# A pipelined scan on one core: the state phase of the second group one slot forward, turned inverses at the end of a half step

## The reference

```python
def step(S, inp):
    r_t, w_t, k_t, v_t, a_t, b_t = inp
    sa = jnp.einsum('zdhij,zdhj->zdhi', S, a_t)
    S = S * w_t[..., None, :] + sa[..., :, None] * b_t[..., None, :] + v_t[..., :, None] * k_t[..., None, :]
    y = jnp.einsum('zdhij,zdhj->zdhi', S, r_t)
    return S, y
```

## Time and profile before

| | us |
|---|---|
| median of 3 runs | 2615.3 (2611.9 to 2617.37) |
| the profiled execution, its own time | 2613.51 |
| its span | 2611.6 |
| TensorE busy | 2464.9 (94%), 28048 instructions |
| TensorE weight loads busy | 2047.2 (78%) |
| VectorE busy | 1210.7 (46%) |
| ScalarE busy | 720.4 (28%) |
| GpSimd busy | 819.8 (31%) |

### The profile page before, as it was taken

How to read it: one execution, slowest core, us unless ns; L and a number is a source line. 1 busy time by engine, 2 the same in 40 slices (tenths; PEclk the granted TensorE clock), 3 DMA queues, 4 the chain that set the end, 5 groups by cost and what they waited for, 6 DMA issues and landing times. The chain is left out here.

```text
span 2611.6 us, 63691 instructions
## 1 busy us (share of the span) xinstructions
PE 2464.9 (94%) x28048; PEld 2047.2 (78%) x28048; DVE 1210.7 (46%) x2468; ACT 720.4 (28%) x1799; POOL 819.8 (31%) x627
## 2 busy tenths in 40 slices
PE   7999999999999599999989989999999999999997
PEld 6785568888888488888777867878888888888885
DVE  4105660000555356566666565554444444444446
ACT  5115651111111355555545432210111001110013
POOL 3322122222332233324333265022333323323234
PEclk9999999999999699999999989999999999999999
DMA  6110011111110100000000052211111111111114
GB/s 165 45 33 18 1 50 73 65 73 73 41 33 25 43 4 4 4 4 4 4 4 4 4 231 92 97 57 35 47 41 41 33 33 49 41 41 33 33 65 145
DMA packets 39087, 123.11 MB, mean 47 GB/s; under 512 B 11424, under 2 KB 11424, under 8 KB 37664
## 3 DMA queue, kind: packets, MB, share of 16 engines
q1 hardware_dynamic: 38816, 119.06, 13.4%
HBM read 96.24 MB, written 20.97 MB: 45 GB/s over the span
## 5 line engine op out<-in xcount | busy, mean ns | idle before, releaser
L2037 DVE TENSOR_TENSOR ff_f<-ff_f,ff_ps 128x512 f32<-128x512 f32 x300 | 205.6, 687 | 173.5 <-PE ff_ps L98 173.5
L1954 ACT ACTIVATE ff_rl<-ff_ps 128x512 f32<-128x512 f32 (+1 forms) x96 | 50.6, 527 | 756.3 <-PE ff_ps L98 756.3
L2056 DVE TENSOR_TENSOR ff_sq<-ff_rl 128x512 f32<-128x512 f32 (+1 forms) x96 | 126.1, 1314 | 273.0 <-ACT ff_rl L1954 272.6
L1823 POOL TENSOR_TENSOR ff_wd0h<-ff_wdr,params 128x1024 fp32r<-128x1024 f32 x16 | 30.3, 1895 | 460.7 <-DMA ff_wdr<-in_w_down 460.7
L996 DVE TENSOR_TENSOR sc_q<-sc_ps,sc_cs 128x128 f32<-128x128 f32 x400 | 97.1, 279 | 163.3 <-PE sc_ps L420 161.4
L436 PE MATMUL sc_ps<-sc_xy,sc_q 64*64 64x64 f32 x3200 | 157.4, 222 | 2.0 <-DVE sc_q L996 1.6
L751 ACT ACTIVATE sc_xy<-sc_ps 128x256 f32<-128x256 f32 x320 | 119.2, 387 | 136.5 <-PE sc_ps L436 134.0
L98 PE MATMUL ff_ps<-hh,ff_wu0h 128*128 128x512 f32 (+1 forms) x384 | 137.0, 357 | 4.7 <-issue 4.7
L432 PE MATMUL sc_ps<-sc_q,sc_xy 64*64 64x64 f32 x2560 | 116.3, 236 | 24.4 <-ACT sc_xy L746 17.4
L98 PE MATMUL ff_ps<-hh,ff_wu0l 128*128 128x512 f32 (+1 forms) x384 | 136.9, 356 | 0.0
L98 PE MATMUL ff_ps<-hl,ff_wu0h 128*128 128x512 f32 (+1 forms) x384 | 136.9, 356 | 0.0
(11 more groups left out here) (306 smaller groups left out, 7059.3 us busy)
## 6 DMA issues: line engine op xcount, KB each, us to landing
ff_wur<-in_w_up SPq DMA_DIRECT2D x32, 512.0 KB, 3.5
ff_wdr<-in_w_down SPq DMA_DIRECT2D x32, 512.0 KB, 4.4
gwr<-in_w_in SPq DMA_DIRECT2D x31, 512.0 KB, 3.2
gm_dram<-gp_gm SPq DMA_DIRECT2D x8, 1280.0 KB, 4.4
ff_m<-gm_dram SPq DMA_DIRECT2D x16, 640.0 KB, 8.2
fr_x<-in_x SPq DMA_DIRECT2D x10, 512.0 KB, 5.4
ff_xs<-in_x SPq DMA_DIRECT2D x10, 512.0 KB, 4.1
x_dram<-ff_xo SPq DMA_DIRECT2D x10, 512.0 KB, 2.9
```

The lines of the kernel that those rows point to most:

```text
L1823: nc.gpsimd.tensor_tensor(high, w_raw[m], zero_like(high, zero), ALU.add).then_inc(high_done, 1)
L1954: nc.scalar.activation(rl[v % 2][:, 0:tn], ps[:, b, 0:tn], ACT.Relu).then_inc(relu, 1)
L2037: nc.vector.tensor_tensor(own, own, ps[:, 4 + v % 4, :], ALU.add).then_inc(added, 1)
L2056: nc.vector.tensor_tensor(sq[v % 2][:, 0:tn], rl[v % 2][:, 0:tn], rl[v % 2][:, 0:tn], ALU.mult).then_inc(squared, 1)
```

## The change

Six things are done, and the arithmetic stays as it is.

1. The two turned inverses of a half step leave its beginning. They are issued at the end of the half step before, behind the last X/Y product; those of the first half step are issued ahead of the loop.
2. Both are copied by one ScalarE instruction. For that the X/Y tiles of two groups lie in one tensor (XYS), and `flipped` counts pairs.
3. The state phase of the second group (sb) moves one slot forward on TensorE, ScalarE and VectorE: state_in ahead of Q of level 2, solved ahead of X/Y of level 2, state_out behind it, outputs behind Q of level 3; VectorE's `state` and `collect` stand in level 3, not 4.
4. The first Q products of both groups stand together, and solved of the group sa stands behind both first X/Y. The gram product of sa stands ahead of Q of level 2, that of sb ahead of Q of level 4; the tokens of sa stand before solved, those of sb before the last X/Y.
5. Side products of piece 1 go from spot 2 to a new spot 5, between outputs and X/Y of level 3; their VectorE half goes from level 4 to 3.
6. The second of the two running sums of the decays goes from level 3 of an odd half step to level 0 of the next one.

```diff
@@ -163,7 +163,8 @@
-        XY = [sb(f"sc_xy{g}", [P, 2, 2, C]) for g in range(GR)]
+        XYS = [sb(f"sc_xy{h}", [P, HALF, 2, 2, C]) for h in range(2)]
+        XY = [XYS[g // HALF][:, g % HALF, :, :, :] for g in range(GR)]
...
+        flips_out = ps[:, GRAM_BANK, 0:HALF * C].rearrange("p (g t) -> p g t", g=HALF)
...
                 if l == 0:
-                    pe.wait_ge(flipped, q * GR + g + 1)
+                    pe.wait_ge(flipped, q * 2 + g // HALF + 1)
...
                     if spot == 2:
                         piece_out(ct, i, 2, GRAM_BANK)
+                    if spot == 5:
                         piece_out(ct, i, 1, TOK_BANK)
...
-                    if spot == 2 and ct + 1 < CT:
+                    if spot == 5 and ct + 1 < CT:
                         pe.wait_ge(sqk_ready, (ct + 2) * NG)
                         by_head(TOK_BANK, nrm, ss_ps)
...
@@ -595,17 +600,15 @@
                 if levels:
                     level_q(q, 0, ga)
+                    level_q(q, 0, gb)
                 if inner:
                     state_in(qs, sa)
                 if levels:
-                    level_q(q, 0, gb)
-                    flip(q, ga)
-                    flip(q, gb)
                     level_xy(q, 0, ga)
+                    level_xy(q, 0, gb)
                 if inner:
                     solved(qs, sa)
                 if levels:
-                    level_xy(q, 0, gb)
                     pe.wait_ge(tok_ready, q * GR + gb + 1)
...
                 if inner:
                     state_in(qs, sb_)
                 if levels:
-                    level_xy(q, 2, gb)
+                    level_q(q, 2, ga)
+                    level_q(q, 2, gb)
                 side(t, 1)
                 if more:
                     by_token(qa, sa)
+                if inner:
+                    solved(qs, sb_)
+                if levels:
+                    level_xy(q, 2, ga)
+                    level_xy(q, 2, gb)
+                if inner:
+                    state_out(qs, sb_)
+                if more:
+                    pe.wait_ge(masked, qa * GR + sa + 1)
+                side(t, 2)
                 if levels:
                     level_q(q, 3, ga)
                     level_q(q, 3, gb)
                 if inner:
-                    solved(qs, sb_)
+                    outputs(qs, sb_)
                 if more:
-                    pe.wait_ge(masked, qa * GR + sa + 1)
                     pe.wait_ge(tok_ready, qa * GR + sa + 1)
-                side(t, 2)
+                side(t, 5)
                 if levels:
                     level_xy(q, 3, ga)
                     level_xy(q, 3, gb)
...
                 if more:
                     gram_products(qa, sb_)
                 if levels:
-                    level_xy(q, 4, ga)
-                    level_xy(q, 4, gb)
+                    level_q(q, 4, ga)
+                    level_q(q, 4, gb)
                 side(t, 4)
                 if more:
                     by_token(qa, sb_)
+                if levels:
+                    level_xy(q, 4, ga)
+                    level_xy(q, 4, gb)
+                if t + 1 < PAIRS:
+                    flip(qa, sa)
+                    flip(qa, sb_)
...
-            def flip_copy(q, g):
-                act.wait_ge(flip_ps, q * GR + g // HALF * HALF + HALF)
-                nc.scalar.activation(XY[g][:, Y_AT, 1, :], flip_out[g], ACT.Copy).then_inc(flipped, 1)
+            def flip_copy(q, h):
+                act.wait_ge(flip_ps, q * GR + h * HALF + HALF)
+                nc.scalar.activation(XYS[h][:, :, Y_AT, 1, :], flips_out, ACT.Copy).then_inc(flipped, 1)
...
+                    if l == 0 and late:
+                        cumulate(q + 1, 1)
...
                     if l == 2 and more:
                         start_group(qa, sa)
-                    if l == 1 and ahead:
-                        half(q + 2, 0)
+                    if l == 3 and inner:
+                        state(qs, sb_)
+                        collect(qs, sb_)
+                    if l == 3:
+                        side(t, 2, GRAM_BANK)
+                        side(t, 1, TOK_BANK)
                     if l == 3 and ahead:
                         half(q + 2, 1)
                         cumulate(q + 2, 0)
-                        cumulate(q + 2, 1)
...
```

More of the change, by code:

```diff
@@ L587, in _ @@
             pe.wait_ge(ta_ready, 2)
+            flip(0, 0)
+            flip(0, 1)
             for t in range(PAIRS + 1):
@@ L617, in _ @@
                     state_out(qs, sa)
+                    outputs(qs, sa)
                 if levels:
@@ L620, in _ @@
                     level_xy(q, 1, gb)
[L621 to L625, removed]
                 if ahead:
@@ L629, in _ @@
                     gram_products(qa, sa)
-                if levels:
-                    level_xy(q, 2, ga)
                 if inner:
@@ L650, in _ @@
                     level_xy(q, 3, gb)
[L651 to L657, removed]
                 side(t, 3)
@@ L777, in _ @@
             decays(1, 1)
+            flip_copy(0, 0)
             for t in range(PAIRS + 1):
@@ L792, in _ @@
                 if levels:
-                    flip_copy(q, ga)
-                    flip_copy(q, gb)
                     level_copy(q, 0, ga)
+                    level_copy(q, 0, gb)
                 if inner:
                     u_copy(qs, sa)
-                if levels:
-                    level_copy(q, 0, gb)
-                if inner:
                     keep(qs, sa)
@@ L804, in _ @@
                     lora_tanh(q + 2, 1)
+                if squares_y and t % 2:
+                    y_square(ct - 1, 1)
                 if levels:
@@ L809, in _ @@
                     decays(q + 1, 0)
[L810 to L813, removed]
                 if inner:
                     p_copy(qs, sb_)
-                if levels:
-                    level_copy(q, 2, gb)
+                    keep(qs, sb_)
                 if more:
@@ L820, in _ @@
                 if inner:
-                    keep(qs, sb_)
+                    u_copy(qs, sb_)
+                if levels:
+                    level_copy(q, 2, ga)
+                    level_copy(q, 2, gb)
                 if late:
@@ L825, in _ @@
                     y_square(ct - 1, 0)
-                if inner:
-                    u_copy(qs, sb_)
-                if levels:
-                    level_copy(q, 3, ga)
-                    level_copy(q, 3, gb)
                 if squares_y and t % 2:
@@ L834, in _ @@
                     k_norm(ct + 1, TOK_BANK)
+                if levels:
+                    level_copy(q, 3, ga)
+                    level_copy(q, 3, gb)
+                if squares_y and t % 2 == 0:
+                    y_square(ct - 1, 2)
                 if squares_k:
@@ L837, in _ @@
                         k_square(ct + 1, p)
+                if more:
+                    token_copy(qa, sb_)
                 if levels:
                     level_copy(q, 4, ga)
-                if squares_y and t % 2 == 0:
-                    y_square(ct - 1, 2)
-                if levels:
                     level_copy(q, 4, gb)
-                if more:
-                    token_copy(qa, sb_)
+                if t + 1 < PAIRS:
+                    flip_copy(qa, sa // HALF)
             def high_half(ct):
@@ L1058, in _ @@
                         collect(qs, sa)
+                    if l == 1 and ahead:
+                        half(q + 2, 0)
                     if l == 2 and more:
                         start_group(qa, sa)
-                    if l == 1 and ahead:
-                        half(q + 2, 0)
+                    if l == 3 and inner:
[4 more added lines that the diff above has]
+                        side(t, 1, TOK_BANK)
                     if l == 3 and ahead:
@@ L1065, in _ @@
                         cumulate(q + 2, 0)
-                        cumulate(q + 2, 1)
-                    if l == 3:
-                        side(t, 2, GRAM_BANK)
-                    if l == 4:
-                        side(t, 1, TOK_BANK)
-                    if l == 4 and inner:
-                        state(qs, sb_)
-                        collect(qs, sb_)
                     if l == 4 and more:
```

## The result

The changed kernel takes 2619.2 us at the median (2615.6 to 2630.1, 14 runs), the kernel before 2614.6 on the same chips (2608.8 to 2617.4, 14 runs): ratio of the means 1.0027, 95% interval 1.0016 to 1.0038, so about 7 us slower by the means and 4.6 by the medians. Its span is 2622.5 against 2611.6. From the first X/Y block to the last output block the scan takes 611.9 us against 605.9; of the other 4.9 us of that pair of spans 4.1 lie behind the scan, where the program is the same.

The account below looks back on a forecast made before the run. TensorE's queue, through the stops at its head, was taken to set the end. The terms 17.8 + 6.1 - 4.1 - 3.2 - 2.5 - 4.9 - 2.5 gave +6.7 us, making 2622 us, range 2617 to 2628.

Parts of the forecast that it names:

- A: Turned inverses at the half-step borders: copy wait goes, but the chain from gram to inverses lengthens; +17.8 us.
- F: VectorE held by GpSimd: three second-group collisions shrink (-2.7), five late tensor_scalars delay less (-2.2); -4.9 us in all.
- B: Side products standing apart in 15 half steps: a second visit costs extra, as do separated sums by head; +6.1 us.
- C: Middle stop behind solved: token copy gets hidden, 0.36 us stays for the first group's mask; -4.1 us.
- E: Late level-2 joins where reciprocals are interspersed: X/Y's wait goes, 0.42 us six times; -2.5 us.
- G: Small Q waits for X/Y copies: level-0 Q without a side product is one block farther away; -2.5 us.
- D: Gram's wait for the variance's root in three half steps goes, since the sum by head stands earlier; -3.2 us.
- 1 (visits free): Side-product visits cost nothing more and the moved waits balance: 2616 us; chance 0.25.
- 3 (chain not lengthened): Chain to the inverses isn't lengthened, as joins lie in the gram's shadow: -23.6 us, 2598; chance 0.08.
- Rival 2: The middle stop goes whole: -17.4 us instead of -4.1, giving 2609; chance 0.15.
- Rival 4: Second group's multiplies fall on GpSimd's two-input instructions at every second border: +1.0 us x 19, 2641; chance 0.10.

Follow-up runs that it names:

- experiment 1: The changed kernel with the two turned inverses back behind both first Q products and state_in, still one ScalarE copy: ratio 1.0020 to the kernel before.
- experiment 2: The kernel before with only the turned inverses moved to the end of a half step, one ScalarE copy for both: ratio 1.0022 to the kernel before.
- experiment 3: The changed kernel with the second group's gram ahead of X/Y of level 3, its VectorE work ahead of the level-4 joins: ratio 1.0006 to the kernel before.
- experiment 4: The changed kernel with sb's gram ahead of X/Y of level 3, tokens behind Q of level 4, mask behind the joins: 2604.8 us, ratio 0.9957 to the kernel before.
- experiment 5: The changed kernel with GpSimd's key multiply and copy ahead of its wait where a new column of tiles begins: ratio 1.0003 to the kernel before.
- experiment 9: Experiment 6 with VectorE's partial reciprocal moved from ahead of the level-4 joins to behind the second group's mask: ratio 0.9948 to the kernel before.
- experiment 7: The changed kernel with side products of piece 1 and sums by head back at spot 2, behind those of piece 2: ratio 1.0013 to the kernel before.
- experiment 6: The changed kernel with the edits of experiment 4 and experiment 5 together: 2600.0 us, ratio 0.9943 to the kernel before.

## Why the prediction was right, step by step

The time (2622 for 2619.2) and the sign came out, and its main mechanism, the longer chain from gram to inverses, stands in the rows of every border and is borne out by experiments 1 to 4. That the sum agrees so well (+6.7 against +6.0 in the scan) is partly luck: large errors cancel in it.

A and F, the border and VectorE held by GpSimd: +17.8 - 4.9 = +12.9 predicted, +13.6 in the table. From gram to X/Y it is 4.51, 0.09 less than predicted. F was wrong in part. Its second half shows in the rows: L873, the tensor_scalar, takes 1.3 to 1.4 us in the five half steps where it took 2.0 to 2.4. The three collisions didn't shrink: L897 takes 1.10, L901 0.64, and the stop is 2.45 us, against a regular 1.29. The rows showed the place, and I took it that an earlier start of GpSimd would leave only its tail there; now the multiply behind it meets the group. What the step didn't price at all is the clock behind these three stops, 3.7 us of the scan by experiment 5. L897 ends 0.15 behind L286, and L887 in experiment 9 0.28 behind L336. The Trainium skill, "SBUF — State Buffer", Who interferes with whom, says that a VectorE instruction with two inputs in SBUF, or in a two-port mode, and a GpSimd one that reads SBUF wait for each other, the second until the first has finished; the trace agrees for L897. Whether L887, with one input, ran in such a mode no trace shows.

B, side products apart: +6.1 predicted, +5.8 in the table and 5.1 taken back by experiment 7. A second visit costs 0.34 (1.83 - 1.49). The Trainium skill, "TensorEngine Tiling (Array Packing)", Key Properties, says that a change of tiling mode drains TensorE, which agrees with a price per visit; no run shows the drain itself.

C, E and G, the small waits in the middle: -9.1 predicted, -18.6 in the table. This is the mis-sized term. I had 0.36 us left ahead of Q of level 3; it is 0.17 (Q starts 0.29 behind state_out's last block, which takes 0.12), and hardly anything in half steps with a side product:

```profile
1193.18 0.33 PE L477 MATMUL sc_ps<-sc_tk 64*64 64x64 f32 x4
...
1193.58 0.28 PE L480 MATMUL sc_ps<-sc_ut,sc_tk 64*64 64x64 f32 x4
1193.87 0.46 PE L422 MATMUL sc_ps<-sc_xy,sc_ai 64*64 64x64 f32 x16
```

And the waits of X/Y behind a gram, 8.3 us in 48 places, I hadn't counted, because each is short and the table of waits hides short ones.

D, the variance's root: -3.2 predicted, -3.6 measured.

Not in the prediction: +8.1 of new waits. State_out now comes only one X/Y pair behind solved, and 31 times it stands for the U copy, mostly some 0.15 us, which ScalarE makes behind the token copy; four times solved waits 0.74 us for the P copy:

```profile
1269.49 0.34 PE L467 MATMUL sc_ps<-sc_pt,sc_xy 64*64 64x64 f32 x8 [0.55 <-ACT sc_pt L764]
```

These took back what C, E and G won beyond my figure: 9.5 more won, 8.1 lost, and 4.7 more inside gram and lora blocks, of which some 2 are lora products at half clock; the rest is spread over the gram products and I have no cause for it. Of the rivals, 1 (visits free) and 3 (chain not lengthened) are refuted by rows. Rival 2 was half right, the middle stop all but went, and was outweighed. Rival 4 (collisions at every second border) came only at the three and, as before the change, once near the end.

## What to carry to other kernels

Before a block is moved away from a stop, add up what stands beside the chain that sets the stop: cover is worth as much as work, and two moves that use the same cover don't add. The cure was to begin the chain one slot earlier and, in the queue of the engine that bounds it, to put only the steps that something waits for ahead of the next consumer; beginning earlier without the second gained a quarter of it. A stop that grew from 1.3 to 2.5 us cost as much again behind it here (1.2 us in it, 1.2 to 1.3 behind it), so read the granted clock behind every longer stop, in more than one trace: the fall doesn't come every time.

## What the runs showed of the hardware that I had not expected

TensorE may run out of instructions. In some dense bursts it stands for 0.55 to 1.3 us in the middle of a block, with "issue" as the cause. From the timeline of the kernel after:

```profile
1080.08 0.28 PE L438 MATMUL sc_ps<-sc_xy,sc_q 64*64 64x64 f32 x2
1081.07 0.27 PE L438 MATMUL sc_ps<-sc_xy,sc_q 64*64 64x64 f32 x2 [0.71 <-issue]
```

and its DMA in the stretch 1078 to 1082, in 40 slices of 0.1 us:

```profile
DMA  0000600000000000000000000000000000000000
...
q8 instruction: 1, 0.02, 1.7%
```

A packet of 16 KB of instructions started at 1078.45 and took 1.07 us; TensorE went on at 1081.07, 1.55 us behind its end. In the scans of all eleven traces I found 60 holes of over 0.55 us inside 64x64 blocks (from one record's start to the next of the same line), and each of them ends 1.25 to 1.6 us behind the end of such a packet, though packets come only every 3.3 to 8.7 us, mostly every 4. Their sum is 1.7 us in the kernel before (2 holes) and 4.6 in the changed one (5), and where they fall differs between kernels with the same TensorE program (experiment 5 has 7). A denser stream doesn't simply have more of them: the fastest versions, of experiments 4, 6 and 9, have 3, 2 and 2, and experiment 7 has 13. No run changed the number or the place of the packets, so that the late packet is the cause is argued from this coincidence, not shown by an edit.
